# Sample scores of two key tiles per matmul with block-diagonal queries, V rows between half panels, masks ahead of the prompt scores, and two steps moved later

## The chip, the cores and the metric

The kernel runs on one core of one Trainium2 chip. The time is the device time of one execution in microseconds; the kernel before took 842.92 us (median of three runs, 841.31 to 843.15). Lower is better. The engines are TensorE (PE in the profile, with its weight loads as PEld), VectorE (DVE), ScalarE (ACT), GpSimd (POOL) and SyncE (SP), which issues most transfers.

## The reference

One layer of a hybrid attention encoder, for 512 prompt tokens and 64 sample tokens. Everything is fp32.

```python
qa, ka, va, qb, kb, vb, gates = split(rmsnorm(x, g_norm1) @ w_in)
oa = sliding_window_attention_with_sinks(qa, ka, va)          # 8 heads of 64, 2 key heads
z = einsum('bqhd,bkhd->bhqk', qb, kb) * HEAD_DIM ** -0.5      # stick-breaking, 8 heads of 64
mask = k_pos[None, :] < q_pos[:, None]
log_1m = where(mask, log_sigmoid(-z), 0)
tail = cumsum(log_1m, reverse=True) - log_1m
ob = einsum('bhqk,bkhd->bqhd', where(mask, exp(log_sigmoid(z) + tail), 0), vb)
merged = sigmoid(gate_a) * (oa @ w_proj_a) + sigmoid(gate_b) * (ob @ w_proj_b)
x = x + merged @ w_out
x = x + square(relu(rmsnorm(x, g_norm2) @ w_up)) @ w_down     # D_FF = 4096
y = rmsnorm(x, g_final)
```

The sample's stick-breaking attention (`sb_sample`) has 64 queries per head against 512 cached keys and the 64 new ones. The new K and V rows are outputs too.

## The kernel before

Activations lie transposed, features on the 128 partitions and the 576 tokens (512 prompt, 64 sample) along the free axis. A large product is a **panel**: 128 output features by 576 tokens, 8 contraction tiles of 128. Each operand is split into a high and a low fp32r part, and a contraction tile takes three products (high by high, high by low, low by high) over two halves of 288 tokens: 6 matmuls per contraction tile, 48 per panel (`mm3`, L1550). A `half_panel` has 4 contraction tiles, 24 matmuls. Each engine runs a program of its own written out by hand, and semaphores tie them together. `tile_out` counts finished panels in halves, `tile_taken` the panels that DVE has copied out of PSUM, `w_lo_ready` the panels whose weights are split.

**The sample's stick-breaking unit.** It runs twice (u = 0, 1), for four heads each time, after the input projection and between the half panels of the first output projection (panels 18 to 21). `sample_scores(u)` first adds a mask (a bf16 matmul of an identity with `smask`). Then, for each of the four heads, it multiplies 64 rows of keys by 64 columns of queries in plain fp32: 4 matmuls for the new keys and 16 for the cached keys `cKT` (4 key blocks by 4 heads). A feature tile of 128 partitions holds two heads, and u picks its upper or lower 64 partitions. Plain fp32 matmuls show as two records each in the trace. DVE and ACT then form magnitudes, exponentials, logarithms and high and low parts (`sp_hi`, `sp_lo`), PE sums them in `tails(u)`, ACT takes the exponential, and `sample_values(u)` multiplies by the V rows. In u = 0 the five groups of four transposes that make the **V rows** (`rows`, L1733) stand so: three groups directly behind the scores, the fourth (`v_rows(3)`) in the middle of half panel (18, 0), the fifth (`v_rows(4)`) before half panel (18, 1). ACT copies them to `vR` in `take_v_rows`, and SP stores `vR` and `kR` when all are there.

**The prompt units.** Eight units (four loops of two) follow, each with `prompt_scores(q)`, two panels, `tails` and the values. The scores are fp32r matmuls of 256, 384 or 512 columns, with bf16 mask matmuls of 128 or 256 columns between them. Three signals `z_out` tell DVE that a bank is complete.

**The second norm.** PE sums the squares by token (L1906), ACT and DVE form the root and DVE spreads it to a tile (`rrep2`); `spread_rms(2, rrep2)` (L1647) turns it with ten matmul records, and stands after 4 of the 8 contraction tiles of panel 51.

**The end.** The down projection is done in quarter products of 12 matmuls (`product`, L1766), which DVE adds to the residual in `take` steps. Output rows are transposed back in `x_rows_out` (L2023). In the last pair of tiles, `x_rows_out(2, 0)` stands between the first product (form 0) and the second (form 6).

Of the kernel before, what the change touches and what calls it, by code (L numbers as in the profile page):

```python
# [54 lines left out]
def build(nc, x_prompt, x_sample, cache_swa_k, cache_swa_v, cache_sb_k, cache_sb_v, rel_table, g1, w_in, sinks,  # L55
          w_pa, w_pb, w_out, g2, w_up, w_down, gf, consts, onehot, y_prompt, y_sample, p_swa_k, p_swa_v,
          p_sb_k, p_sb_v, s_swa_k, s_swa_v, s_sb_k, s_sb_v):
    with ExitStack() as ctx:
# [481 lines left out]
        def _(act):  # L540
# [153 lines left out]
            def sb_logs(u, order, wid):  # L694

                for n, bank in enumerate(order):
# [5 lines left out]
                    if isinstance(u, int) and u == 0 and n:  # L702
                        take_v_rows(n - 1)
# [31 lines left out]
            for u in range(2):  # L735
                sb_logs(u, SAMPLE_ORDER, SAMPLE_W)
                if u == 0:
                    take_v_rows(2)
                    take_v_rows(3)
                    take_v_rows(4)  # L740
                round_next(4, 2 * u)
                if u:
# [5 lines left out]
                nc.scalar.activation(ob_hi[u * HD:(u + 1) * HD, :, SEQ:TOK], att[0:HD, 3, 0:4 * NEW].rearrange("p (h n) -> p h n", h=4),  # L748
                                     ACT.Copy).then_inc(sbo_hi, 1)
# [153 lines left out]
        def _(dve):  # L903
# [252 lines left out]
            for u in range(2):  # L1156
# [20 lines left out]
                for n in range(1, 4):  # L1177
# [3 lines left out]
                nc.vector.tensor_tensor(ob_lo[u * HD:(u + 1) * HD, :, SEQ:TOK], att[0:HD, 3, 0:4 * NEW].rearrange("p (h n) -> p h n", h=4),  # L1181
                                        ob_hi[u * HD:(u + 1) * HD, :, SEQ:TOK].bitcast(F32), ALU.subtract).then_inc(sbo_taken, 1)
# [362 lines left out]
        def _(pe):  # L1545
# [598 lines left out]
```

## Time and profile before

| | |
|---|---|
| median of three runs | 842.92 us (841.31 to 843.15) |
| the profiled execution | 847.74 us |
| its span, first to last instruction | 845.9 us |
| mean granted TensorE clock | 0.989 |
| PE busy | 833.9 us, 99% of the span |
| DVE busy | 621.5 us, 73% |
| ACT busy | 391.2 us, 46% |
| POOL busy | 293.3 us, 35% |

The span ends with some 8 us in which PE has no more work: the last rows are scaled and stored. A row of a timeline gives start, duration, engine, line, operation, out<-in, shapes and how many records were merged. A matmul's duration holds a fixed part of its pipeline, so the cost of one in a row of alike records is the distance between starts. It is read as the row's duration less that of one record, divided by the number of records less one.

### The profile page before, as it was taken

How to read it: one execution, taken by the hardware profiler on the slowest of the kernel's cores; microseconds unless marked ns; L12 is line 12 of the kernel's file. 1: busy time of each engine (PE TensorE's matmuls, PEld its weight loads, DVE VectorE, ACT ScalarE, POOL GpSimd, SP SyncE). 2: the span in 40 equal slices, each digit the busy share in tenths (PEclk: the TensorE clock that was granted, in tenths of full speed). 3: DMA queues.
4: the chain of work that ended last, by engine and by line, in shares of the span. 5: the costliest groups of instructions: out<-in, count | busy, mean ns of one | idle time of the engine just before them, and what ended most of it. 6: DMA issues, size and time to landing. Idle time of an engine off the chain costs nothing.

```text
span 845.9 us, 16088 instructions
## 1 busy us (share of the span) xinstructions
PE 833.9 (99%) x6245; PEld 815.6 (96%) x6245; DVE 621.5 (73%) x1069; ACT 391.2 (46%) x666; POOL 293.3 (35%) x213
## 2 busy tenths in 40 slices
PE   9999999999999999999999999999999999999996
PEld 7999999999999999999999999999999999999995
DVE  5597876245688999967336889488975889489896
ACT  5667774233468677553343333323433333333532
POOL 2463222312535555245334400542025400452330
PEclk9999999988999999999999999999999999999998
DMA  8752112441111122143232213413133212322203
GB/s 278 253 166 72 51 51 66 147 162 51 51 51 50 50 71 79 50 162 117 60 99 87 65 50 100 149 52 96 51 100 107 92 50 93 120 84 61 87 2 113
DMA packets 68449, 78.18 MB, mean 92 GB/s; under 512 B 2552, under 2 KB 65072, under 8 KB 68016
## 3 DMA queue, kind: packets, MB, share of 16 engines
q1 hardware_dynamic: 68080, 76.92, 28.3%
q8 instruction: 32, 0.52, 0.3%
q10 hardware_dynamic: 320, 0.60, 0.2%
q14 instruction: 17, 0.14, 0.1%
HBM read 70.15 MB, written 8.93 MB: 93 GB/s over the span
## 4 chain that ended last, share of the span: by engine, by line
PE 91%; DVE 6%; issue 1%; ACT 1%; DMA 1%; ACTq 0%; DVEq 0%
PE pan L1550 58%; PE pan L1766 12%; PE att L1766 12%; PE att L1704 1%; PE att L1677 1%; PE pan L1606 1%; PE att L1694 1%; PE att L1550 1%; DVE xT L1383 1%; PE att L1845 1%; DMA grow<-in_g 1%; PE pan L1639 1%; PE att L1733 0%; DVE sq_sum L1482 0%; DVE x_out L1469 0%
## 5 line engine op out<-in xcount | busy, mean ns | idle before, releaser
L468 POOL TENSOR_TENSOR w_lo<-raw,w_hi 128x512 fp32r<-128x512 f32 x160 | 221.1, 1406 | 437.5 <-ACT w_hi L810 183.6
L1550 PE MATMUL pan<-a_hi,w_hi 128*128 128x288 f32 x624 | 134.3, 297 | 0.0
L1550 PE MATMUL pan<-a_lo,w_hi 128*128 128x288 f32 x624 | 133.8, 295 | 0.0
L1550 PE MATMUL pan<-a_hi,w_lo 128*128 128x288 f32 x624 | 133.2, 295 | 0.0
L1550 PE MATMUL pan<-h_hi,w_hi 128*128 128x288 f32 x512 | 111.1, 299 | 0.0
L1550 PE MATMUL pan<-h_lo,w_hi 128*128 128x288 f32 x512 | 109.5, 295 | 0.0
L1550 PE MATMUL pan<-h_hi,w_lo 128*128 128x288 f32 x512 | 108.3, 293 | 0.0
L1550 PEld LDWEIGHTS pan<-a_hi,w_lo 128*128 128x128 f32 x624 | 100.8, 188 | 0.0
L1550 PEld LDWEIGHTS pan<-a_hi,w_hi 128*128 128x128 f32 x624 | 99.4, 188 | 0.3
L1550 PEld LDWEIGHTS pan<-a_lo,w_hi 128*128 128x128 f32 x624 | 99.4, 188 | 0.0
L1766 PE MATMUL pan<-F_hi,w_hi 128*128 128x288 f32 x320 | 96.3, 301 | 0.0
L1766 PE MATMUL pan<-F_lo,w_hi 128*128 128x288 f32 x320 | 94.7, 296 | 0.0
L1766 PE MATMUL pan<-F_hi,w_lo 128*128 128x288 f32 x320 | 94.3, 295 | 0.0
L1550 PEld LDWEIGHTS pan<-h_lo,w_hi 128*128 128x128 f32 x512 | 83.7, 190 | 0.0
L1550 PEld LDWEIGHTS pan<-h_hi,w_lo 128*128 128x128 f32 x512 | 82.6, 188 | 0.0
L1550 PEld LDWEIGHTS pan<-h_hi,w_hi 128*128 128x128 f32 x512 | 81.2, 188 | 0.1
L1766 PEld LDWEIGHTS pan<-F_hi,w_hi 128*128 128x128 f32 x320 | 60.1, 188 | 1.2 <-DVE F_lo L1303 0.7
L1766 PEld LDWEIGHTS pan<-F_hi,w_lo 128*128 128x128 f32 x320 | 60.2, 188 | 0.0
L810 ACT ACTIVATE w_hi<-raw 128x1024 fp32r<-128x1024 f32 x28 | 29.7, 1061 | 65.8 <-PE pan L1550 43.9
L1766 PEld LDWEIGHTS pan<-F_lo,w_hi 128*128 128x128 f32 x320 | 60.1, 188 | 0.0
L1283 DVE TENSOR_TENSOR up_t<-pan,rms 128x576 f32<-128x576 f32 x32 | 24.1, 754 | 36.5 <-PE pan L1550 36.3
L545 ACT ACTIVATE w_hi<-raw 128x1024 fp32r<-128x1024 f32 x32 | 33.4, 1056 | 28.0 <-PE pan L1550 27.8
(281 smaller groups left out, 1790.1 us busy)
## 6 DMA issues: line engine op xcount, KB each, us to landing
raw<-in_w_in SPq DMA_DIRECT2D x34, 512.0 KB, 4.8
raw<-in_w_up SPq DMA_DIRECT2D x32, 512.0 KB, 4.5
raw<-in_w_down SPq DMA_DIRECT2D x32, 512.0 KB, 4.6
raw<-in_w_out SPq DMA_DIRECT2D x8, 512.0 KB, 4.0
x_spill<-xT SPq DMA_DIRECT2D x1, 2304.0 KB, 7.1
xT<-x_spill SPq DMA_DIRECT2D x1, 2304.0 KB, 10.6
x_rows<-in_x_prompt SPq DMA_DIRECT2D x4, 512.0 KB, 7.1
raw<-in_w_pa SPq DMA_DIRECT2D x4, 512.0 KB, 4.1
```

Source lines behind the costliest of these rows:

```text
L468: last = nc.gpsimd.tensor_tensor(w_lo[:, slot, k:k + 4, :], raw[:, rs, k:k + 4, j * P:(j + 1) * P], w_hi[:, slot, k:k + 4, :].bitcast(F32) ...
L545: nc.scalar.activation(w_hi[:, slot4(j), :, :], raw[:, 1 - j // 2, :, (j % 2) * P:(j % 2 + 1) * P], ACT.Copy).then_inc(w_hi_ready, 1)
L810: nc.scalar.activation(w_hi[:, slot4(n % 4), :, :], raw[:, 1 - n // 2 % 2, :, (n % 2) * P:(n % 2 + 1) * P], ACT.Copy).then_inc(w_hi_ready, 1)
L1283: nc.vector.tensor_tensor(halves(up_t[:, b, :]), pan_out(b), halves(rms[:]), ALU.mult).then_inc(tile_taken, 2)
L1383: nc.vector.tensor_tensor(xT[:, tile, cols], xT[:, tile, cols], bank, op).then_inc(taken, 1)
L1550: got = nc.tensor.matmul(out[:, h, 0:HALF], w, x[:, h * HALF:(h + 1) * HALF], start=first and n == 0, stop=last and n == 2)
L1606: nc.tensor.matmul(pan[:, j, h, 0:HALF], w_hi[:, j, k, :], x[:, k, h * HALF:(h + 1) * HALF], start=k == 0 and x is a_hi, stop=False)
L1639: got = nc.tensor.matmul(pan[:, j, h, 0:HALF], w_lo[:, j, k, :], a_hi[:, k, h * HALF:(h + 1) * HALF], start=False, stop=k == KT - 1)
L1677: got = nc.tensor.matmul(att[0:width(t), r, e * 256:(e + 1) * 256], qa_st[:, e, pair, t * P:t * P + width(t)], part[:, pair // 2, k0:k0 + ...
L1694: got = nc.tensor.transpose(att[0:kn, 2, c:c + w], s_sw[0:w, r, e, kb * P:kb * P + kn], ident[0:w, 0:w])
L1704: got = nc.tensor.matmul(att[0:HD, 3, 0:256].rearrange("p (e n) -> p e n", e=2)[:, :, 0:width(t)], va_st[0:kn, vt, g // 10, v_part, :], p_ ...
L1766: return nc.tensor.matmul(out, lhsT, rhs, start=start, stop=stop, skip_group_check=True)
```

## The change

- In `sample_scores` the four 64-row matmuls of a step become two 128-row ones. A new tile `qz` holds, for each of the four feature tiles, 128 columns: the 64 queries of the tile's first head on the upper 64 partitions with zeros below, and those of the second head on the lower 64 with zeros above. A unit now takes the two heads of two feature tiles (heads 4u to 4u+3) and not one head of each of four. DVE fills `qz` by two memsets and two copies, ahead of the copies of the K rows.
- The result of the values goes out in two pieces, on ACT and on DVE.
- The V rows: three groups in the middle of half panel (18, 0), the fourth before half panel (18, 1), the fifth in its middle. ACT takes the first later in its program.
- In `prompt_scores` all masks stand ahead of the scores.
- `spread_rms(2)` stands after 5 contraction tiles of panel 51.
- `x_rows_out(2, 0)` stands behind the form 6 product.

```diff
+        qz = work("qz", [P, 4, P], 98976)
+        def sample_out(e):
+            return att[0:HD, 3, 0:4 * NEW].rearrange("p (h e n) -> p e h n", h=2, e=2)[:, e, :, :]
@@ scalar
-                    if isinstance(u, int) and u == 0 and n:
-                        take_v_rows(n - 1)
+                    if isinstance(u, int) and u == 0 and n == 2:
+                        take_v_rows(0)
...
-                    take_v_rows(2)
-                    take_v_rows(3)
-                    take_v_rows(4)
+                    for n in range(1, TT + 1):
+                        take_v_rows(n)
...
-                nc.scalar.activation(ob_hi[u * HD:(u + 1) * HD, :, SEQ:TOK], att[0:HD, 3, 0:4 * NEW].rearrange("p (h n) -> p h n", h=4),
-                                     ACT.Copy).then_inc(sbo_hi, 1)
+                for e in range(2):
+                    last = nc.scalar.activation(ob_hi[e * HD:(e + 1) * HD, 2 * u:2 * u + 2, SEQ:TOK], sample_out(e), ACT.Copy)
+                last.then_inc(sbo_hi, 1)
@@ vector
             dve.wait_ge(stored, 6 * 16)
+            dve.wait_ge(tile_taken, 2 * KB)
+            for e in range(2):
+                own, other = slice(e * HD, (e + 1) * HD), slice((1 - e) * HD, (2 - e) * HD)
+                nc.vector.memset(qz[other, :, e * NEW:(e + 1) * NEW], 0.0)
+                last = nc.vector.tensor_copy(qz[own, :, e * NEW:(e + 1) * NEW], qkvT[own, QB:QB + 4, SEQ:TOK])
+            last.then_inc(qz_ready, 1)
...
@@ tensor, sample_scores
-                for h in range(4):
-                    got = acc(att[0:NEW, 2, h * NEW:(h + 1) * NEW], qkvT[rows, KB + h, SEQ:TOK], qkvT[rows, QB + h, SEQ:TOK], stop=h == 3)
+                for h in range(2):
+                    got = acc(att[0:NEW, 2, h * P:(h + 1) * P], qkvT[:, KB + 2 * u + h, SEQ:TOK], qz[:, 2 * u + h, :], stop=h == 1)
...
-                        for h in range(4):
-                            got = acc(att[:, bank, c % 512 + h * NEW:c % 512 + (h + 1) * NEW], cKT[rows, h, kb * P:(kb + 1) * P],
-                                      qkvT[rows, QB + h, SEQ:TOK], start=kb % 2 == 0 and h == 0, stop=kb % 2 == 1 and h == 3)
+                        for h in range(2):
+                            got = acc(att[:, bank, c % 512 + h * P:c % 512 + (h + 1) * P], cKT[:, 2 * u + h, kb * P:(kb + 1) * P],
+                                      qz[:, 2 * u + h, :], start=kb % 2 == 0 and h == 0, stop=kb % 2 == 1 and h == 1)
@@ tensor, half panels of u = 0
-                half_panel(18 + 2 * u, 0, slot4(2 * u), oa_hi, oa_lo, middle=None if u else lambda: v_rows(3))
+                half_panel(18 + 2 * u, 0, slot4(2 * u), oa_hi, oa_lo, middle=None if u else first_v_rows)
                 if u == 0:
-                    v_rows(4)
+                    v_rows(3)
                     pe.wait_ge(vrows_ready, 3)
-                half_panel(18 + 2 * u, 1, slot4(2 * u), oa_hi, oa_lo)
+                half_panel(18 + 2 * u, 1, slot4(2 * u), oa_hi, oa_lo, middle=None if u else lambda: v_rows(4))
@@ tensor, prompt_scores
-                qk(2, att[:, 1, 0:256], 256, start=True)
-                acc(att[:, 1, 0:P], ident_b[:], strict)
+                acc(att[:, 1, 0:P], ident_b[:], strict, start=True)
                 acc(att[:, 1, 256:512], ident_b[:], mask2[:])
+                acc(att[:, 2, 0:P], ident_b[:], strict, start=True)
+                acc(att[:, 0, 0:P], ident_b[:], strict, start=True)
+                qk(2, att[:, 1, 0:256], 256)
...
-            panel(first_panel(12) + 1, slot4(1), 1, h_hi, h_lo, part=(0, 4))
+            panel(first_panel(12) + 1, slot4(1), 1, h_hi, h_lo, part=(0, 5))
             spread_rms(2, rrep2)
...
             product(last_a, 2, 0, 0).then_inc(prod_out, 1)
-            x_rows_out(2, 0)
             last_taken(-2)
             pe.wait_ge(*quarter_low(3, 3, 3))
             product(att[:, 0, 0:HALF], 0, 0, 6).then_inc(prod_out, 1)
+            x_rows_out(2, 0)
```

PE's program before, at the scores of u = 0. `qkvT` holds queries, keys and values; L1766 is the helper of the scores, L1733 the V rows, L1550 the panels.

```order
L1766 MATMUL att<-smask,ident_b 128x256
L1766 MATMUL att<-qkvT 64x64 x4
L1766 MATMUL att<-qkvT,cKT 128x64 x16
L1733 MATMUL att<-ident,qkvT 64x128 x4
L1733 MATMUL pan<-ident,qkvT 128x128 x8
L1550 MATMUL pan<-oa_hi,w_hi 128x288 x2
L1550 MATMUL pan<-oa_lo,w_hi 128x288 x2
```

The same place in the changed kernel, where the three lines are L1781, L1748 and L1565.

```order
L1781 MATMUL att<-smask,ident_b 128x256
L1781 MATMUL att<-qz,qkvT 64x128 x2
L1781 MATMUL att<-qz,cKT 128x128 x8
L1565 MATMUL pan<-oa_hi,w_hi 128x288 x2
L1565 MATMUL pan<-oa_lo,w_hi 128x288 x2
L1565 MATMUL pan<-oa_hi,w_lo 128x288 x2
```

Twenty matmuls of 64 columns have become ten of 128 columns, and the twelve transposes behind them have gone; they follow after two contraction tiles (12 matmuls) of the half panel.

PE's program before, at the scores of a prompt unit (q_hi, q_lo and k_st are the parts of queries and keys, mask_60 the mask).

```order
L1766 MATMUL att<-q_hi_87,k_st_85 128x256
L1766 MATMUL att<-q_lo_89,k_st_85 128x256
L1766 MATMUL att<-mask_60,ident_b 128x128
L1766 MATMUL att<-mask_60,ident_b 128x256
L1766 MATMUL att<-q_hi_87,k_st_85 128x256
L1766 MATMUL att<-q_lo_89,k_st_85 128x256
L1766 MATMUL att<-q_hi_87,k_st_85 128x384
L1766 MATMUL att<-q_lo_89,k_st_85 128x384
L1766 MATMUL att<-mask_60,ident_b 128x128
L1766 MATMUL att<-q_hi_87,k_st_85 128x512
L1766 MATMUL att<-q_lo_89,k_st_85 128x512
L1766 MATMUL att<-mask_60,ident_b 128x128
```

And in the changed kernel.

```order
L1781 MATMUL att<-mask_60,ident_b 128x128
L1781 MATMUL att<-mask_60,ident_b 128x256
L1781 MATMUL att<-mask_60,ident_b 128x128 x2
L1781 MATMUL att<-q_hi_88,k_st_86 128x256
L1781 MATMUL att<-q_lo_90,k_st_86 128x256
L1781 MATMUL att<-q_hi_88,k_st_86 128x256
L1781 MATMUL att<-q_lo_90,k_st_86 128x256
L1781 MATMUL att<-q_hi_88,k_st_86 128x384
L1781 MATMUL att<-q_lo_90,k_st_86 128x384
L1781 MATMUL att<-q_hi_88,k_st_86 128x512
L1781 MATMUL att<-q_lo_90,k_st_86 128x512
```

The same twelve matmuls, with one change from bf16 to fp32r in place of three.

DVE's program before, where the K rows are copied (kR), between two copies of panels (L973).

```order
L1103 MEMSET vR 64x512
L1111 COPY kR<-att 128x512 x2
L973 SCALAR_TENSOR_TENSOR qkvT<-pan,qscale,rms 128x576
L1111 COPY kR<-att 128x512 x2
L1111 COPY kR<-att 64x512
```

And in the changed kernel.

```order
L1115 MEMSET qz 64x4x64
L1116 COPY qz<-qkvT 64x4x64
L1115 MEMSET qz 64x4x64
L1116 COPY qz<-qkvT 64x4x64
L1123 COPY kR<-att 128x512 x2
L979 SCALAR_TENSOR_TENSOR qkvT<-pan,qscale,rms 128x576
```

Four instructions of 64 partitions by 256 elements stand between the wait for the stores and the first copy of K rows.

## Rows read from the trace of the kernel before

**Rows 1.** The page: busy time, granted clock by slice, chain; longest piece of the chain.

```profile
PE 833.9 (99%) x6245; PEld 815.6 (96%) x6245; DVE 621.5 (73%) x1069; ACT 391.2 (46%) x666; POOL 293.3 (35%) x213
...
PEclk9999999988999999999999999999999999999998
...
PE 91%; DVE 6%; issue 1%; ACT 1%; DMA 1%; ACTq 0%; DVEq 0%
...
364.59 82.74 PE pan L1550 x624
```

**Rows 2.** Windows: length, busy by engine (PE first), then granted clock, DMA, GB/s.

```profile
168.50:169.00 0.50, 0.50 (x7) 0.50 (x5) 0.40 (x1) 0.07 (x1) 0.50 (x1) 0.87 0.00 0
169.00:169.50 0.50, 0.50 (x4) 0.50 (x4) 0.00 (x0) 0.50 (x2) 0.23 (x1) 0.50 0.00 0
...
175.50:176.00 0.50, 0.50 (x5) 0.50 (x5) 0.47 (x2) 0.00 (x0) 0.00 (x0) 0.81 0.12 33
...
196.00:196.50 0.50, 0.50 (x5) 0.50 (x5) 0.27 (x1) 0.20 (x1) 0.50 (x1) 0.67 0.00 0
...
203.00:203.50 0.50, 0.50 (x5) 0.50 (x5) 0.02 (x1) 0.00 (x0) 0.00 (x0) 1.00 0.00 0
```

**Rows 3.** Timeline of PE at both sample scores.

```profile
165.35 0.28 PE L1766 MATMUL att<-smask,ident_b 128*128 128x256 bf16 x1
...
166.17 4.66 PE L1766 MATMUL att<-qkvT,cKT 64*128 64x64 f32 x32
170.76 1.06 PE L1733 MATMUL att<-ident,qkvT 128*64 128x128 f32 x4
...
192.73 0.28 PE L1766 MATMUL att<-smask,ident_b 128*128 128x256 bf16 x1
...
198.20 0.85 PE L1550 MATMUL pan<-oa_hi,w_hi 128*128 128x288 f32 x2
```

**Rows 4.** Timeline of PE, plain fp32 records with all 128 rows.

```profile
161.29 1.03 PE L1751 MATMUL att<-ident,ckR 128*128 128x128 f32 x8
...
189.19 0.63 PE L1845 MATMUL att<-sp,cV 128*64 128x64 f32 x8
```

**Rows 5.** Timeline of DVE where `qz` is to be filled.

```profile
146.63 1.29 DVE L1111 COPY kR<-att 128x512 f32<-128x512 f32 x2 [2.21 <-DMA out_s_swa_v<-vaR]
149.83 0.82 DVE L973 SCALAR_TENSOR_TENSOR qkvT<-pan,qscale,rms 128x576 f32<-128x576 f32 x1 [1.91 <-PE pan L1550]
```

**Rows 6.** Timeline of DVE in u = 1: third magnitude, copy of panel (20, 0).

```profile
198.31 0.69 DVE L1125 TENSOR_SCALAR sp<-att 128x512 int32<-128x512 int32 x1 [2.04 <-PE att L1766]
...
203.83 0.76 DVE L1160 COPY m_a<-pan 128x576 f32<-128x576 f32 x1 [0.81 <-PE pan L1550]
```

**Rows 7.** Timeline of PE in a prompt unit, behind a mask matmul.

```profile
219.00 0.48 PE L1766 MATMUL att<-q_hi,k_st 128*128 128x512 f32 x1
219.32 0.40 PE L1766 MATMUL att<-q_lo,k_st 128*128 128x512 f32 x1
```

**Rows 8.** PE's longest wait in the prompt units; waits of PEld (us, times, longest).

```profile
321.56 0.44 PE L1766 MATMUL att<-sp_hi,suffix 128*128 128x384 f32 x1 [0.74 <-DVE sp_lo L1147]
...
PEld att L1766 <- DVE sp_lo L1147: 1.8, 6, 0.9
```

**Rows 9.** Timeline of PE at the second norm's spread.

```profile
451.27 0.42 PE L1550 MATMUL pan<-h_hi,w_lo 128*128 128x288 f32 x2
...
452.17 1.52 PE L1647 MATMUL att<-ident,rrep 128*128 128x128 f32 x10 [0.48 <-DVE rrep L960]
```

**Rows 10.** Timelines of PE and DVE at the last pair.

```profile
823.09 0.65 PE L2023 MATMUL att<-ident,xT 128*128 128x128 f32 x4 [1.01 <-DVE xT L1383]
...
825.18 0.29 PE L1766 MATMUL pan<-F_hi,w_hi 128*128 128x288 f32 x1
...
822.59 0.45 DVE L1383 TENSOR_TENSOR xT<-xT,pan 128x288 f32<-128x288 f32 x1
...
824.22 0.45 DVE L1383 TENSOR_TENSOR xT<-xT,pan 128x288 f32<-128x288 f32 x1
```

More of the change, by code:

```diff
@@ L202, in build @@
         krows_out, vrows_out, vrows_ready, krows_ready = sem("krows_out"), sem("vrows_out"), sem("vrows_ready"), sem("krows_ready")
+        qz_ready = sem("qz_ready")
         csb_in, ckT_out, ckT_ready = sem("csb_in"), sem("ckT_out"), sem("ckT_ready")
@@ L1180, in _ @@
                 dve.wait_ge(stored, (6 + 4) * 16)
-                nc.vector.tensor_tensor(ob_lo[u * HD:(u + 1) * HD, :, SEQ:TOK], att[0:HD, 3, 0:4 * NEW].rearrange("p (h n) -> p h n", h=4),
-                                        ob_hi[u * HD:(u + 1) * HD, :, SEQ:TOK].bitcast(F32), ALU.subtract).then_inc(sbo_taken, 1)
+                for e in range(2):
+                    own = slice(e * HD, (e + 1) * HD)
+                    last = nc.vector.tensor_tensor(ob_lo[own, 2 * u:2 * u + 2, SEQ:TOK], sample_out(e), ob_hi[own, 2 * u:2 * u + 2, SEQ:TOK].bitcast(F32),
+                                                   ALU.subtract)
+                last.then_inc(sbo_taken, 1)
             def take_gate(i, j):
@@ L1768, in sample_scores @@
             def sample_scores(u):
-                rows = slice(u * HD, (u + 1) * HD)
                 acc(att[:, 2, 0:4 * NEW], ident_b[:], smask[:], start=True)
-                for h in range(4):
-                    got = acc(att[0:NEW, 2, h * NEW:(h + 1) * NEW], qkvT[rows, KB + h, SEQ:TOK], qkvT[rows, QB + h, SEQ:TOK], stop=h == 3)
+                for h in range(2):
+                    got = acc(att[0:NEW, 2, h * P:(h + 1) * P], qkvT[:, KB + 2 * u + h, SEQ:TOK], qz[:, 2 * u + h, :], stop=h == 1)
                 got.then_inc(z_out, 1)
@@ L1813, in _ @@
                     pe.wait_ge(ckT_ready, 4)
+                    pe.wait_ge(qz_ready, 1)
                 else:
@@ L1816, in _, with first_v_rows @@
                 sample_scores(u)
-                if u == 0:
+                def first_v_rows():
                     pe.wait_ge(tile_taken, 2 * QKV)
@@ L1840, in sample_values @@
                     for h in range(4):
-                        c = (2 * h + u) * HD
+                        c = (4 * u + h) * HD
                         for kb in range(5):
@@ L1858, in prompt_scores @@
                 strict = mask2[:, P:2 * P]
-                qk(2, att[:, 1, 0:256], 256, start=True)
-                acc(att[:, 1, 0:P], ident_b[:], strict)
+                acc(att[:, 1, 0:P], ident_b[:], strict, start=True)
                 acc(att[:, 1, 256:512], ident_b[:], mask2[:])
+                acc(att[:, 2, 0:P], ident_b[:], strict, start=True)
+                acc(att[:, 0, 0:P], ident_b[:], strict, start=True)
+                qk(2, att[:, 1, 0:256], 256)
                 qk(3, att[:, 1, 256:512], 256, stop=True).then_inc(z_out, 1)
-                qk(1, att[:, 2, 0:384], 128, start=True)
-                acc(att[:, 2, 0:P], ident_b[:], strict, stop=True).then_inc(z_out, 1)
-                qk(0, att[:, 0, :], 0, start=True)
-                acc(att[:, 0, 0:P], ident_b[:], strict, stop=True).then_inc(z_out, 1)
+                qk(1, att[:, 2, 0:384], 128, stop=True).then_inc(z_out, 1)
+                qk(0, att[:, 0, :], 0, stop=True).then_inc(z_out, 1)
             pe.wait_ge(tile_taken, 44)
@@ L1912, in _ @@
             feature_sums(1)
-            panel(first_panel(12) + 1, slot4(1), 1, h_hi, h_lo, part=(0, 4))
+            panel(first_panel(12) + 1, slot4(1), 1, h_hi, h_lo, part=(0, 5))
             spread_rms(2, rrep2)
-            panel(first_panel(12) + 1, slot4(1), 1, h_hi, h_lo, part=(4, KT))
+            panel(first_panel(12) + 1, slot4(1), 1, h_hi, h_lo, part=(5, KT))
             for n in range(2, 8):
```

## The prediction

> **What bounds the kernel now.** I read the page first: busy shares, granted clock by slice, the chain that ended last. PE is busy for 833.9 us, 99% of the span, and holds 91% of the chain [rows 1]. So a microsecond counts if PE loses or gains it, and the work of the others matters only where PE waits for it. The same group gives the yardstick: a run of 624 panel matmuls takes 82.74 us, 0.1326 us each, so 12 take 1.59 us and a half panel of 24 takes 3.18 us.
>
> Next, the clock. The row by slice dips in slices 9 and 10, and again in the last, where PE's work is over [rows 1]. Windows of half a microsecond place the two dips. With PE busy 0.50 of 0.50, the granted clock is 0.87 in the window from 168.50 and 0.50 in the next, so it fell at 168.87; by 0.81 in the window from 175.50 it rose at 175.69. It fell again at 196.17 and was back at 203.00 [rows 2]. That is twice 6.8 us at 1.2 GHz instead of 2.4. The timeline shows what PE did before each fall: sample scores, from 165.35 and from 192.73, thus 3.5 us of matmuls that fill 64 rows of the array [rows 3].
>
> **Sample scores: fewer records.** At u = 0 the scores last from 165.35 to 170.76, 5.41 us; at u = 1 from 192.73 to 198.20, 5.47 us [rows 3]. The clock was halved for 1.89 and 2.03 us of these, so at full clock they are 4.46 and 4.45 us. Now the new form. No row shows a 128-row fp32 score of 128 columns. The nearest are the transposes with all 128 rows and 128 columns: eight records in 1.03 us, the last 0.27, so (1.03 - 0.27) / 7 = 0.109 us apart [rows 4]. The low side is the fp32 records of 64 weight columns in the values: (0.63 - 0.22) / 7 = 0.059 [rows 4]. The old scores' cached part gives the high side: 32 records in 4.66 us with 1.89 at half clock, so (4.66 - 0.27 - 0.95) / 31 = 0.111 for only 64 columns [rows 3]; twice that for twice the columns would be 0.22. I take 0.109, since both operands have the transposes' shape. With 4 + 16 records for 8 + 32: 0.22 for the mask + 20 x 0.109 = 2.40 us. PE gains 2.06 + 2.05 = **4.1 us**, between 0 (0.22 a record) and 6.1.
>
> **Sample scores: the clock.** If it stays up, each 6.8 us stretch becomes 3.4 us: **6.8 us** in both. The reason to think so: the new scores are shorter (2.4 us against 3.5 us before the fall), fill all 128 rows, and panel matmuls follow them (at u = 0 twelve transposes did). Also, the values are a stretch of fp32 records too, 40 of them at 0.059 each, 2.4 us with all rows filled [rows 4], and ended shortly before the second scores without a fall before 196.17 [rows 2]. Bounds: 0 to 6.8.
>
> The Trainium skill, in "TensorE: Matmul & The Clock Gate" (Part 1: The HAM clock gate), says that the clock is granted by how busy the array has been and falls after an idle stretch. The falls here came with PE busy in all of every window [rows 2], so busy in the profile's sense isn't what is counted. By the page's wording, scores that keep PE just as busy in their new form would be treated as before, and the clock term is 0, which is a rival below.
>
> **What the filling of `qz` costs.** Four DVE instructions of 64 partitions by 256 elements. A copy of 128x512 takes 0.64 us by two in 1.29 [rows 5]; half the columns is about 0.3, so 1.2 in all. DVE starts the K rows at 146.63, and before the next panel copy at 149.83 it was idle for 1.91 us [rows 5], which covers it; PE needs `qz` some 17 us later. Cost 0; without the cover the K copies come 1.2 us late and PE would wait up to that.
>
> **V rows, and the waits behind the scores.** The twenty transposes stay the same. With the scores 2.1 us shorter and the clock up, PE reaches everything behind them earlier, and DVE and ACT must follow. For u = 0 I set out the chain with the durations above: scores end at 167.75, two contraction tiles, V rows to 170.6, and so on to the tails at 179.5; DVE's copy of half panel (18, 0) waits for the fifth V group. Behind that PE has 12 panel matmuls, 1.59 us, before it needs the bank, and the copy takes 0.76 [rows 6]: some 0.5 us to spare, signals included. The splits then have the whole half panel (19, 0), 3.18 us. No wait. For u = 1 it is tighter. Half panel (21, 0) needs the copy of (20, 0). Before, DVE started the third magnitude at 198.31 and that copy at 203.83, of which 0.81 was idle: 4.71 us of work [rows 6]. Now the magnitudes come right behind the two result pieces: the third starts 3.3 us after the scores start, so the copy ends at 3.3 + 4.7 + 0.76 = 8.8 us. PE is there at 2.40 + 2 x 3.18 = 8.76. I take a **loss of 0.1 us**, 0 to 0.7.
>
> **Masks ahead.** A matmul behind a mask shows 0.48 us against 0.40 for the same shape behind fp32r [rows 7]: its weight load isn't hidden, 0.08. Three such changes a unit become one. The wide mask's costs about nothing, so one 0.08 goes, and a unit that begins behind a wait starts with a cheaper bf16 load. That is 0.1 us x 8 units. But in three units DVE, late by its own backlog, ends the wait (0.74 us at 321.56, and 1.8 us in 6 times [rows 8]), and what PE saves ahead of such a wait is given back. Five units: **0.5 us**, 0 to 0.9. The first signal `z_out` comes 0.2 us later, the last earlier; where DVE is late it isn't waiting for it.
>
> **The norm's spread.** The last two panel records start at 451.27 and end their slot at 451.53, the spread starts at 452.17 [rows 9]: 0.64 us lost. Six more matmuls are 0.80, so the spread would start at 452.33 with `rrep2` there. **0.6 us**, 0.4 at least. DVE gets its result 0.17 us later, and PE needs the tile it frees only a panel later.
>
> **The last row transposes.** PE waits 1.01 us for DVE's `take` that starts at 822.59, and the third product starts at 825.18 [rows 10]. In the new order form 6 runs in that gap, from 821.93 to 823.5, the transposes to 824.0. The third product then waits for the take that starts at 824.22, DVE being busy throughout, and ends at 824.67 [rows 10]: it starts at 824.7. **0.45 us** and not 1.0, range 0.2 to 1.0. The wait moves from the transposes to the product.
>
> **Sum.** 4.1 + 6.8 + 0.5 + 0.6 + 0.45 - 0.1 = 12.35 us. Against its own time the profiled execution goes from 847.74 to 835.4. It was 4.8 us above the median of the runs, 842.92; the same gain gives **830.6 us**.
>
> **Rivals.** (1) The clock term is missing (20%): it falls again, or it fell in the profiled execution alone. For: the page's rule above, and the 4.8 us between profile and median. Against: the three runs lie within 1.84 us, so none of them differs from the rest by two such falls, and the shorter scores fill the array. Gain 5.55: 837.4 us. With one of two falls left, 834.0.
> (2) DVE and ACT don't follow, and their chain from the scores to the splits sets the start of the tails (7%). The scores and the clock give PE 5.5 us in each unit, all of it ahead of the tails. If one unit's chain kept its old times, 5.5 of it would be lost: 836.1 us. For: the chain is long, with 4.71 us of DVE work behind the third signal of u = 1 [rows 6], and has only 0.1 us or less to spare there. Against: its inputs are PE's results, which all move.
> (3) Slower (3%): the 128-column records are the price, and the clock falls as before. The old scores' records took 0.111 us, and twice that at half clock. If a record of the new shape took 0.25, a unit's scores would be 0.22 + 20 x 0.25 = 5.2 us, 0.75 more than 4.45, twice 1.5, and the 1.45 of the three small edits would be gone: from there the change loses. At 0.32 it is 842.92 + 2 x 2.15 - 1.45 = 845.8 us. Against: the 0.109 of the transposes [rows 4].
>
> The change could also fail to do what it says only in the three small edits, which the range holds.
>
> **Chances.** Forecast with its own range (829.3 to 832.5) 68%, rival (1) 20%, rival (2) 7%, rival (3) 3%, better than 829.3 2%. A range from 829.2 to 837.5 holds some 85%, and the unknown costs reach across it. A difference of 0.2% (1.7 us) is about what a measurement can tell from no change. Only rival (3), and a mix of both (1) and (2), come near that: faster 0.95, same 0.03, slower 0.02.
>
> **What would show it.** In the new profile: granted clock 1.00 from 165 to 200 us (term of 6.8); score stretches of 2.4 us, with records 0.109 apart; tails of u = 0 near 179.5; a wait of PE by DVE's copy before half panel (21, 0) of at most 0.2 us; one slow fp32r matmul a prompt unit, with the waits for `sp_lo` at 0.1 more each; no idle PE before the spread; 0.7 us of idle PE between the last transposes and the third product. Clock windows at 0.50 behind the new scores would make the forecast wrong by 3.4 us each, score records above 0.15 by 0.8 us or more.

## The result and the profile after

The changed kernel takes **836.17 us** (median of four runs, 836.07 to 836.72). Beside it the kernel before took 843.03 (four runs, 841.31 to 843.46), a ratio of 0.9913 with a 95% interval of 0.9887 to 0.994. The gain is 6.9 us. The forecast was 830.6 us: the sign was right, the result lies in the wide range (829.2 to 837.5), and the likeliest value was 5.6 us too low. Yet the two profiled executions differ by 847.74 - 836.16 = 11.58 us, close to the forecast sum of 12.35.

The page after: busy time, clock by slice, the chain by engine (to [rows 1]).

```profile
PE 822.9 (99%) x6205; PEld 807.0 (97%) x6205; DVE 624.6 (75%) x1075; ACT 391.4 (47%) x668; POOL 294.6 (35%) x213
...
PEclk9999999999999999999999999999999999999998
...
PE 88%; DVE 9%; issue 2%; ACT 1%; DVEq 0%; ACTq 0%
```

PE is busy for 11.0 us less, and the dip of slices 9 and 10 is gone. Windows of 5 us around the scores of u = 0 and behind those of u = 1 (columns as in [rows 2]) have the clock at 1.00:

```profile
165.00:170.00 5.00, 5.00 (x41) 4.61 (x40) 2.95 (x5) 3.17 (x6) 2.52 (x2) 1.00 0.00 0
170.00:175.00 5.00, 5.00 (x43) 5.00 (x41) 3.08 (x6) 3.02 (x6) 0.00 (x0) 1.00 0.66 210
...
193.00:198.00 5.00, 5.00 (x39) 4.83 (x38) 4.79 (x10) 1.66 (x3) 0.00 (x0) 1.00 0.63 210
```

PE's timeline in the same execution, from the scores to the tails of both units, the first prompt unit, the norm's spread and the last pair (to [rows 3, 7, 9, 10]):

```profile
165.59 0.28 PE L1781 MATMUL att<-smask,ident_b 128*128 128x256 bf16 x1
165.80 0.65 PE L1781 MATMUL att<-qz,qkvT 128*64 128x128 f32 x4
166.38 2.05 PE L1781 MATMUL att<-qz,cKT 128*128 128x128 f32 x16
168.19 0.51 PE L1565 MATMUL pan<-oa_hi,w_hi 128*128 128x288 f32 x2
...
169.86 0.60 PE L1748 MATMUL att<-ident,qkvT 128*64 128x128 f32 x4
...
179.96 0.28 PE L1781 MATMUL att<-sp_hi,suffix 128*128 128x256 f32 x1
...
187.94 0.28 PE L1781 MATMUL att<-smask,ident_b 128*128 128x256 bf16 x1
...
201.40 0.28 PE L1781 MATMUL att<-sp_lo,prefix 128*128 128x256 f32 x1
201.69 0.39 PE L1781 MATMUL att<-sp_hi,suffix 128*128 128x256 f32 x1
...
208.47 0.45 PE L1781 MATMUL att<-mask,ident_b 128*128 128x128 bf16 x4
208.72 0.36 PE L1781 MATMUL att<-q_hi,k_st 128*128 128x256 f32 x1
...
442.42 1.41 PE L1662 MATMUL att<-ident,rrep 128*128 128x128 f32 x10
443.76 0.53 PE L1565 MATMUL pan<-h_hi,w_hi 128*128 128x288 f32 x2
...
812.53 0.60 PE L2039 MATMUL att<-ident,xT 128*128 128x128 f32 x4
813.73 0.40 PE L1781 MATMUL pan<-F_hi,w_hi 128*128 128x288 f32 x1 [0.59 <-DVE xT L1398]
```

The scores take 2.6 us (165.59 to 168.19), and their cached records are (2.05 - 0.27) / 15 = 0.119 us apart. The tails of u = 0 begin 14.37 us behind the mask that opens the scores; in the profile of before it was 19.4. Inside the tails of u = 1 there is a new gap at 201.69, where matmuls otherwise follow 0.12 us apart. The spread has no wait in front of it, and in the last pair 0.59 us of wait stand ahead of the third product. So the profile shows nearly what was forecast. Why did the time not show it?

### The profile page after: what moved, and what is told of

Read it like the earlier page. It is cut to its first block, busy times and chain, and to the rows that moved or that the text cites. A ratio compares the mean times of both kernels' runs of the same rounds, so it can differ in the third digit from the quotient of the medians.

```text
span 834.3 us, 16017 instructions
## 1 busy us (share of the span) xinstructions
PE 822.9 (99%) x6205; PEld 807.0 (97%) x6205; DVE 624.6 (75%) x1075; ACT 391.4 (47%) x668; POOL 294.6 (35%) x213
## 4 chain that ended last, share of the span: by engine, by line
PE 88%; DVE 9%; issue 2%; ACT 1%; DVEq 0%; ACTq 0%
PE pan L1565 56%; PE pan L1781 12%; PE att L1781 10%; PE att L1719 1%; PE att L1692 1%; PE pan L1621 1%; DVE sp_lo L1159 1%; PE att L1709 1%; PE att L1565 1%; DVE sp_hi L1157 1%; DVE xT L1398 1%; PE pan L1601 1%; PE att L1861 1%; PE pan L1654 1%; DVE ob_lo L1221 1%
## 5 line engine op out<-in xcount | busy, mean ns | idle before, releaser
L1565 PE MATMUL pan<-a_lo,w_hi 128*128 128x288 f32 x624 | 133.8, 295 | 0.0
L1565 PE MATMUL pan<-a_hi,w_hi 128*128 128x288 f32 x624 | 133.8, 296 | 0.0
L1565 PE MATMUL pan<-a_hi,w_lo 128*128 128x288 f32 x624 | 133.1, 294 | 0.0
L1565 PE MATMUL pan<-h_hi,w_hi 128*128 128x288 f32 x512 | 110.5, 298 | 0.0
L1565 PE MATMUL pan<-h_lo,w_hi 128*128 128x288 f32 x512 | 109.5, 295 | 0.0
L1565 PE MATMUL pan<-h_hi,w_lo 128*128 128x288 f32 x512 | 108.5, 293 | 0.0
L1565 PEld LDWEIGHTS pan<-a_hi,w_hi 128*128 128x128 f32 x624 | 99.9, 188 | 1.0
L1565 PEld LDWEIGHTS pan<-a_hi,w_lo 128*128 128x128 f32 x624 | 100.8, 188 | 0.0
L1565 PEld LDWEIGHTS pan<-a_lo,w_hi 128*128 128x128 f32 x624 | 99.6, 188 | 0.0
L1781 PE MATMUL pan<-F_hi,w_hi 128*128 128x288 f32 x320 | 96.4, 301 | 0.6 <-DVE xT L1398 0.6
L1781 PE MATMUL pan<-F_lo,w_hi 128*128 128x288 f32 x320 | 94.7, 296 | 0.0
L1781 PE MATMUL pan<-F_hi,w_lo 128*128 128x288 f32 x320 | 94.3, 295 | 0.0
L1565 PEld LDWEIGHTS pan<-h_lo,w_hi 128*128 128x128 f32 x512 | 83.2, 189 | 0.0
L1565 PEld LDWEIGHTS pan<-h_hi,w_lo 128*128 128x128 f32 x512 | 82.7, 188 | 0.0
L1565 PEld LDWEIGHTS pan<-h_hi,w_hi 128*128 128x128 f32 x512 | 81.4, 188 | 0.1
L1781 PEld LDWEIGHTS pan<-F_hi,w_hi 128*128 128x128 f32 x320 | 60.1, 188 | 2.0 <-DVE xT L1398 1.1
L1781 PEld LDWEIGHTS pan<-F_hi,w_lo 128*128 128x128 f32 x320 | 60.2, 188 | 0.0
L1781 PEld LDWEIGHTS pan<-F_lo,w_hi 128*128 128x128 f32 x320 | 60.1, 188 | 0.0
```

The lines of the kernel that those rows point to most:

```text
L1565: got = nc.tensor.matmul(out[:, h, 0:HALF], w, x[:, h * HALF:(h + 1) * HALF], start=first and n == 0, stop=last and n == 2)
L1781: return nc.tensor.matmul(out, lhsT, rhs, start=start, stop=stop, skip_group_check=True)
```

## Experiments

Each was timed beside the kernel before. All times are medians, with the lowest and the highest. A **fall** is a stretch in which the granted clock is half (1.2 GHz in place of 2.4).

### 1. The kernel before, unchanged

No edit.

> The kernel before, unchanged, to see the clock of each of its executions. Theory A (the two stretches at half clock belong to some executions, the profiled one among them; most timed ones have none or one, or shorter ones): the mean granted clock of most executions is above the 0.989 of the profiled one, up to the 0.996 of the kernel after, and span and clock move together, 1% of clock for some 8 us of span; executions without a fall take 840.9 us (847.74 - 6.8), with one fall 844.3. Theory B (every execution has both falls): the clock is 0.989 in all of them, whatever their time, and the 4.8 us between the profiled execution and the median are something else.

**Measured:** 843.59 us (841.98 to 847.80, 12 runs), against 843.46 for before: ratio 1.001 (0.9986 to 1.0033). With the runs of before beside all the experiments there are 99 executions of this one kernel, with the span and the mean clock of each. They form three groups:

| executions | time | median | mean granted clock |
|---|---|---|---|
| 13 | 841.18 to 842.02 | 841.63 | 0.996 to 0.997 |
| 53 | 842.59 to 844.70 | 843.30 | 0.993 to 0.996 |
| 33 | 846.23 to 848.74 | 847.63 | 0.988 to 0.991 |

The profiled execution of this run was one of the middle group (843.17 us). Its windows of half a microsecond show one fall only, and that a short one:

```profile
170.00:170.50 0.50, 0.50 (x6) 0.43 (x6) 0.17 (x1) 0.20 (x1) 0.00 (x0) 0.99 0.00 0
170.50:171.00 0.50, 0.50 (x5) 0.46 (x3) 0.50 (x2) 0.00 (x0) 0.00 (x0) 0.50 0.57 59
...
173.50:174.00 0.50, 0.50 (x4) 0.50 (x4) 0.45 (x2) 0.50 (x2) 0.00 (x0) 0.60 1.08 367
174.00:174.50 0.50, 0.50 (x6) 0.50 (x6) 0.45 (x2) 0.21 (x1) 0.00 (x0) 1.00 0.43 131
```

It lasts from 170.5 to 173.9, 3.4 us at half rate, and costs 1.7: the distance between the first two medians (843.30 - 841.63). The two falls of [rows 2] cost 6.8 by their rows; the third median lies 6.0 above the first. Only single executions were profiled; that the others of a group had the same falls is read from their time and mean clock. Theory A holds and theory B falls. Theory A allowed for shorter falls, but had no time for them, and they are the commonest: a short fall at u = 0, and none at u = 1.

The u = 1 of this execution is undisturbed, and so gives what no row of before could. From the chain of the end (start, length, line):

```profile
191.70 4.44 PE att L1766 x41
196.15 9.72 PE pan L1550 x72
...
211.17 2.48 PE att L1845 x40
...
215.51 6.54 PE pan L1550 x49
```

### 2. The new scores alone

```diff
+        qz = work("qz", [P, 4, P], 98976)
...
-                for h in range(4):
-                    got = acc(att[0:NEW, 2, h * NEW:(h + 1) * NEW], qkvT[rows, KB + h, SEQ:TOK], qkvT[rows, QB + h, SEQ:TOK], stop=h == 3)
+                for h in range(2):
+                    got = acc(att[0:NEW, 2, h * P:(h + 1) * P], qkvT[:, KB + 2 * u + h, SEQ:TOK], qz[:, 2 * u + h, :], stop=h == 1)
```

> The kernel before with the block-diagonal sample scores alone (qz, 128-row score records, the outputs' head order); V rows, masks, spread and last rows as before. Both theories: the scores' stretch is 2.69 us as in the kernel after, against 4.45 at full clock, so 1.76 a unit, 3.5 us in both. Theory A (the records are a real gain, and the 6.8 us of the clock are a gain only against executions that had the falls): clock 0.996 in every execution, time about 837.4 (840.9 - 3.5), 5.5 us under the median of before and over 10 us under its profiled time. Theory C (the move of the V rows is what keeps the clock up, not the scores' form): clock falls to half behind the scores of u = 0 or u = 1 still, mean clock 0.993 or less, time 840 or more.

**Measured:** 838.08 us (837.89 to 838.46, 7 runs), ratio 0.992 (0.9891 to 0.9949), clock 0.996 or 0.997 in every execution. The V rows stand in their old place, so theory C falls. Against executions of before without a fall (called undisturbed from here on) the gain is 841.63 - 838.08 = 3.55 us, against the median of all some 5.4.

### 3. All but the scores

```diff
-                for h in range(2):
-                    got = acc(att[0:NEW, 2, h * P:(h + 1) * P], qkvT[:, KB + 2 * u + h, SEQ:TOK], qz[:, 2 * u + h, :], stop=h == 1)
+                for h in range(4):
+                    got = acc(att[0:NEW, 2, h * NEW:(h + 1) * NEW], qkvT[rows, KB + h, SEQ:TOK], qkvT[rows, QB + h, SEQ:TOK], stop=h == 3)
```

(against the kernel after; the cached part and the outputs likewise)

> The kernel after with the old sample scores (64-row records, no qz): V rows between steps, masks ahead, spread and last rows later are as in after. Theory A: the three small edits give 1.5 us (0.5 masks, 0.6 spread, 0.45 last rows) and the V rows nothing, so executions without a fall take 839.4 us, and falls behind the scores are as frequent as in before. Theory C (the V rows keep the clock up): no fall in any execution, clock 0.996, 839.4 in all. If the V rows' place costs PE something by itself, the time is above 839.4 at clock 0.996.

**Measured:** 843.52 us (839.85 to 846.13, 12 runs), ratio 0.9988 (0.9963 to 1.0014). Only two executions kept 0.997 (839.85 and 839.99); the profiled one has a fall from 168.4 to 175.3, which began before its scores ended at 171.2. The four other edits without the scores bring 1.7 us to an undisturbed execution, and don't hold the clock.

### 4. The three small edits alone

```diff
-            panel(first_panel(12) + 1, slot4(1), 1, h_hi, h_lo, part=(0, 4))
+            panel(first_panel(12) + 1, slot4(1), 1, h_hi, h_lo, part=(0, 5))
```

(with the masks' and the last rows' edits as in the change)

> The kernel before with the three small edits alone: masks ahead of the prompt scores, the second norm's spread two panel steps later, the last row transposes behind form 6. By the rows of the two traces: masks 0.4 to 0.5 us, spread 0.6, last rows 0.45, together 1.5 us, so 1.5 under a run of before with the same clock (839.4 without a fall). Rival: later waits take the masks' share back, and the sum is 1.0. A difference to the kernel after's gain of more than 5.4 us is then the scores' and the clock's.

**Measured:** 842.01 us (839.81 to 847.09, 12 runs), ratio 0.9983 (0.9958 to 1.0009); its two executions at 0.997 took 839.81 and 839.94. That is again 1.7 us under 841.63, and the same as experiment 3: the V rows' move is worth nothing measurable, as far as two executions of each can tell.

### 5. All 128 rows, but as many matmuls as before

```diff
-                for h in range(2):
-                    got = acc(att[0:NEW, 2, h * P:(h + 1) * P], qkvT[:, KB + 2 * u + h, SEQ:TOK], qz[:, 2 * u + h, :], stop=h == 1)
+                for h in range(4):
+                    k, e = 2 * u + h // 2, slice(h % 2 * NEW, (h % 2 + 1) * NEW)
+                    got = acc(att[0:NEW, 2, h * NEW:(h + 1) * NEW], qkvT[:, KB + k, SEQ:TOK], qz[:, k, e], stop=h == 3)
```

(against experiment 2; the cached part likewise)

> The block-diagonal kernel of the run before (all else as in before), with each score matmul cut into two of 64 query columns, so that the array's 128 rows are filled but there are as many records as in before (8 and 32 a unit). Price: if a record costs by its columns, 40 x 0.06 = 2.4 us a unit and the time is 838; if a record costs the same 0.11 whatever the columns, the scores take 4.45 us as in before, 3.5 us more than with 20 records, 841.4 at full clock. Clock: theory R (the 64 rows are what let it fall): clock 0.996 in every execution. Theory L (the length of the fp32 stretch is what lets it fall, however many rows): falls as in before, in most executions, mean clock down to 0.989, times spread over 6 us.

**Measured:** 841.38 us (841.05 to 841.65, 12 runs), ratio 0.9962 (0.9946 to 0.9979), clock 0.996 to 0.998 in all twelve. The cached scores in PE's timeline, and below them those of the undisturbed u = 1 of experiment 1, with 64 rows:

```profile
166.31 3.79 PE L1782 MATMUL att<-qz,cKT 128*128 128x64 f32 x32
...
192.36 3.78 PE L1766 MATMUL att<-qkvT,cKT 64*128 64x64 f32 x32
```

This is the experiment that decides. The stretch is as long as before (4.45 us), with as many matmuls, and of the scores only the rows differ (half of the 128 meet the zeros of `qz`). By time and mean clock 86 of 99 executions with 64 rows have a fall, 21 of the 23 timed beside this experiment, and of 12 with 128 rows none. And it prices the record: (3.79 - 0.27) / 31 = 0.114 us with 64 query columns, whether 128 rows are filled or 64, and 0.119 with 128. Half the matmuls at 128 columns are therefore nearly half the time, 841.38 - 838.08 = 3.3 us.

### 6. As few matmuls, but 64 rows

```diff
-                    got = acc(att[0:NEW, 2, h * P:(h + 1) * P], qkvT[:, KB + 2 * u + h, SEQ:TOK], qz[:, 2 * u + h, :], stop=h == 1)
+                    got = acc(att[0:NEW, 2, h * P:(h + 1) * P], qkvT[0:HD, KB + 2 * u + h, SEQ:TOK], qz[0:HD, 2 * u + h, :], stop=h == 1)
```

(against experiment 2; the cached part likewise)

> The block-diagonal kernel with the score matmuls cut to the first 64 rows: 20 records a unit of 64 rows and 128 columns (every second head's scores are left out, so the output differs). Both theories: 2.69 us a unit as with 128 rows, 838.0 us if the clock holds. Theory R (64 rows): the clock can fall, some executions 2 to 7 us longer with mean clock 0.989 to 0.995. Theory L (length): as short as the block-diagonal form, so no fall in any execution, and all within 1 us of 838.0.

**Measured:** 838.16 us (837.74 to 838.50, 6 runs), ratio 0.9923 (0.9894 to 0.9951), clock 0.996 or 0.997 in all six. No fall: 64 rows for 2.7 us did not bring one. So theory R in its plain form (64 rows are enough) is not borne out. But this edit changes two things against the kernel before: the stretch is shorter, and each matmul has 128 query columns in place of 64. Which of the two kept the clock up is not separated here. Six executions don't exclude a rare fall either.

### 7 and 8. Both kinds of scores issued twice

```diff
+                sample_scores(u, False)
                 sample_scores(u)
```

> The block-diagonal kernel with every score matmul of the sample issued twice (the first pass is written over): 2 x 2.69 = 5.4 us of 128-row fp32 scores a unit, longer than the old ones' 4.45. Theory R: no fall, clock 0.996 in every execution, time 838.0 + 5.4 = 843.4 with a spread of 1 us. Theory L: falls in at least as many executions as in before, 845 to 850 us, clock down to 0.989.

> The kernel before with every score matmul of the sample issued twice (the first pass is written over): 8.9 us of 64-row scores a unit at full clock. Both theories: the clock falls more often or for longer than in before: without a fall it would be 841.3 + 8.9 = 850.2 us, with one or two 853 to 858 us, and the shortest executions, those without a fall, become rare or go. If the times stay near 850.2 at clock 0.996, neither rows nor length of the scores is the cause.

**Measured, 128 rows:** 843.29 us (842.65 to 843.62, 12 runs), ratio 0.9985 (0.9966 to 1.0003), clock 0.996 to 0.998 in all: 5.36 us of fp32 records with all rows filled, longer than the old scores, and no fall.

**Measured, 64 rows:** 862.49 us (859.96 to 863.21, 6 runs), ratio 1.0201 (1.017 to 1.0233), clock 0.981 to 0.985: a long fall in every execution. Both have the same place in the kernel, but not the same length. The windows of the profiled execution with 64 rows:

```profile
169.50:170.00 0.50, 0.50 (x7) 0.50 (x6) 0.00 (x0) 0.00 (x0) 0.03 (x1) 1.00 0.00 0
170.00:170.50 0.50, 0.50 (x5) 0.31 (x5) 0.00 (x0) 0.00 (x0) 0.00 (x0) 0.89 0.00 0
...
184.00:184.50 0.50, 0.50 (x6) 0.50 (x5) 0.47 (x2) 0.00 (x0) 0.00 (x0) 0.96 0.00 0
```

The clock is at half from 170.4 to 184.0, with PE busy 0.50 of 0.50, and again from 204.5 to 218.2. I had expected 853 to 858: each fall is 13.6 us long here and costs 6.8, and two of them with the 8.9 us of matmuls make 841.6 + 8.9 + 13.6 = 864, which is near the 863.07 of this execution.

### 9 and 10. The new gap in the tails of u = 1

DVE in the kernel after, third addition and split of u = 1:

```profile
196.20 0.75 DVE L1172 COPY m_a<-pan 128x576 f32<-128x576 f32 x1
...
198.50 1.43 DVE L1157 CAST sp_hi<-sp 128x512 fp32r<-128x512 f32 x1
199.97 1.67 DVE L1159 TENSOR_TENSOR sp_lo<-sp,sp_hi 128x512 fp32r<-128x512 f32 x1
201.56 1.41 DVE L1172 COPY m_a<-pan 128x576 f32<-128x576 f32 x2
```

The same two operations took 0.43 and 0.69 us one bank earlier. POOL at that time:

```profile
198.37 2.72 POOL L474 TENSOR_TENSOR w_lo<-raw,w_hi 128x512 fp32r<-128x512 f32 x2 [6.52 <-ACT w_hi L551]
```

PE waits for `sp_lo`, which ends at 201.64. The first edit (9) moves the work that lets POOL start:

```diff
-                round_next(4, 2 * u)
-                if u:
+                if u == 0:
+                    round_next(4, 0)
+                else:
                     stage_high(0, 0)
                 sb_weights(u, SAMPLE_ORDER, SAMPLE_W)
+                if u:
+                    round_next(4, 2)
```

The second (10) adds, on DVE:

```diff
-                        if n == 2:
-                            take_proj(4)
                         added = sb_add(u, n, SAMPLE_ORDER, SAMPLE_W, SAMPLE_ADDS, added)
+                        if n == 1:
+                            take_proj(4)
                         sb_split(u, n, SAMPLE_ORDER, SAMPLE_W)
```

> The kernel after with one move on ACT: at u = 1 the rounding of the next weight panel (w_hi, at 197.23) stands behind the tails' exponentials and not ahead of them, so POOL's split of that panel (198.37, 2.72 us) comes some 6 us later. Theory P (DVE's sp_hi and sp_lo at 198.50 took 1.43 and 1.67 us in place of 0.43 and 0.69 because POOL's split ran beside them): both are back at 0.43 and 0.69, PE's wait inside the tails of u = 1 (201.40 to 201.69) is gone, and PE gains 0.2 us: 835.9 against 836.17. Rival: the two are slow for another reason and stay at 1.4 and 1.7, or the later rounding costs PE a wait for w_lo at panel 22, over 836.2.

> The same, and DVE's copy of half panel (20, 0) one step earlier, ahead of the second split and not of the third addition. If PE's wait of 0.18 us ahead of half panel (21, 0) (its 72 matmuls take 9.72 us in place of 9.53) is for that copy alone, the piece takes 9.53, and the second split ends 0.7 us later without PE noticing: 0.4 us under the kernel after with both moves, 835.8. Rival: the bank is late by something else and the piece stays at 9.7; then 835.95.

**Measured:** 839.80 us (838.50 to 840.46, 12 runs) with the first, 839.81 (838.25 to 841.33, 12 runs) with both: ratios 0.9951 (0.9934 to 0.9968) and 0.9939 (0.9918 to 0.9959). Both are 3.3 us slower than the kernel after (836.48 on the same chip, experiment 11), where a gain of 0.2 to 0.4 was expected. The splits are back at 0.43 and 0.69 us, so theory P is right in what it says of DVE, but its gain is swamped: POOL's chain to `q_lo` comes late for the first prompt unit. PE in the profiled executions of 9 and of 10, then the windows of 10 there:

```profile
210.63 0.45 PE L1784 MATMUL att<-mask,ident_b 128*128 128x128 bf16 x4 [2.57 <-POOL q_lo L497]
...
210.23 0.71 PE L1784 MATMUL att<-mask,ident_b 128*128 128x128 bf16 x4 [2.56 <-POOL q_lo L497]
```

```profile
208.00:209.00 1.00, 0.00 (x0) 0.00 (x0) 0.56 (x2) 0.97 (x3) 1.00 (x2) 1.00 0.00 0
209.00:210.00 1.00, 0.00 (x0) 0.00 (x0) 0.00 (x0) 0.99 (x2) 1.00 (x1) 0.88 0.00 0
210.00:211.00 1.00, 0.77 (x5) 0.71 (x6) 0.00 (x0) 0.07 (x1) 0.92 (x2) 0.50 0.00 0
```

PE waits for 2.56 us in 10, and before it resumes at 210.23 the clock falls, this time with PE idle: the 12 score matmuls behind the wait take 3.12 us. In the profiled execution of 9 the wait is as long (2.57 us) and there is no fall: the same 12 take 1.79 us. So one and the same wait can bring a fall or not. By the mean clock there was one in 8 of 12 executions of 10 (0.994 or 0.995, 839.53 us and more; the other four, at 0.996, took 838.25 to 838.87), and in at least 5 of 12 of 9.

### 11 and 12. The kernel after again, and the two moves with POOL in time

```diff
+                if u:
+                    act.wait_ge(tile_out, 2 * (first_panel(4) + 6) - 6)
+                    stage_high(0, 0)
                 round_next(4, 2 * u)
-                if u:
-                    stage_high(0, 0)
```

(experiment 12, with the DVE edit of 10)

> The kernel after, unchanged, beside the other two on the same chip: 836.2 us with the clock at 0.996 in every execution, since the 128-row scores do not let it fall; all within 0.7 us. If a fall shows in one of them (clock under 0.995, 838 us or more), the 128 rows only make it rarer.

> The kernel after with two moves at u = 1: ACT makes the parts of k_st and q_hi first (behind the wait for the same half panel as before) and rounds the weight panel behind them, so POOL's split starts at about 200.2 and not 198.4, and its q_lo for the first prompt unit ends near 206.9, ahead of the 208.4 at which PE wants it; DVE copies half panel (20, 0) ahead of the second split. Theory P (POOL beside DVE's splits stretched them, and the copy alone held up half panel (21, 0)): DVE's sp_hi and sp_lo are at 0.43 and 0.69 us, the 72 matmuls take 9.53 and not 9.72, no wait inside the tails, and the start of the first prompt unit keeps its time behind the values: 0.2 + 0.2 = 0.4 us under after's 836.2 to 836.5, so 835.9. Rival: as in the two moves tried before, POOL's chain to q_lo comes late and PE waits for it; then 836.5 or more, and a wait of 1 us or more lets the clock fall as well.

**Measured:** the kernel after took 836.48 us (836.08 to 836.80, 6 runs), ratio 0.9912 (0.9883 to 0.994), clock 0.996 to 0.998. The version of 12 took **835.85 us** (835.61 to 835.93, 6 runs), ratio to before 0.9897 (0.9871 to 0.9924). Its slowest execution is faster than the fastest of after's ten, but it ran on another chip than any of these, so the traces must carry the comparison: from the start of the scores of u = 0 to the panels of the first prompt unit the chain takes 44.05 us here and 44.51 in the kernel after. Its DVE and its chain:

```profile
198.31 0.43 DVE L1158 CAST sp_hi<-sp 128x512 fp32r<-128x512 f32 x1
198.78 0.69 DVE L1160 TENSOR_TENSOR sp_lo<-sp,sp_hi 128x512 fp32r<-128x512 f32 x1
```

```profile
190.59 9.52 PE pan L1566 x72
200.11 2.13 PE att L1782 x18
202.24 3.17 PE pan L1566 x24
205.41 2.48 PE att L1862 x40
207.88 1.72 PE att L1782 x12
```

POOL's split now starts at 199.94, behind DVE's. The piece of 72 is back at 9.52, the gap is gone, and the prompt unit follows the values without a wait.

## Why the forecast was right and where it failed

**The step that failed** is the last of the sum: "the same gain gives 830.6 us". It carried the profiled execution's gain over to the median. The clock term of 6.8 us was read rightly from its rows and is gone as forecast; but by time and mean clock only a third of the executions of before (33 of 99) lose about that much. The median one has the short fall of 1.7. Put that in place of 6.8 and the sum of the forecast is 7.25, 835.7 us. The profile's own 4.8 us above the median said so, and I had it in rival (1), "it fell in the profiled execution alone", at 20%. What I held against it was that the three runs lie within 1.84 us, "so none of them differs from the rest by two such falls". That is true, and also what one sees if none of the three has them. The result, 836.17, lies nearer to rival (1)'s 837.4 than to the forecast, and it is in the stated range only because the range reached out to that rival. That it meets rival (2)'s 836.1 is chance: the 5.5 us that rival (2) takes away were to be lost to DVE and ACT in one unit, and the kernel after loses 0.27 there.

**Score records.** I took 0.109 us, the transposes' distance; it is 0.119. The undisturbed old scores of experiment 1 are 4.44 us in the chain against 2.69 now: 1.75 a unit, 3.5 for 4.1. The low bound of 0.059 was out of reach: it belongs to records with 64 weight columns and 64 moving ones. The first V group has 64 weight columns too, but 128 moving ones, and takes (0.60 - 0.27) / 3 = 0.11.

**Why the clock stays up.** "Fill all 128 rows" was right: shown by 5 against 1. Experiment 7 bears it out, since 5.36 us with 128 rows are longer than the old scores' 4.45 and brought no fall; against 8 it differs in rows and in length. "Shorter" is in part argued. With one and the same form of matmul, 4.4 us (1) mostly brought a fall and 8.9 us (8) a long one each time. But 6, the only run with 64 rows and a short stretch, has 128 query columns a matmul as well; a stretch of 2.7 us in the old form was not run. The panel matmuls behind the scores matter little: in 3 they stand there too, and the clock fell before PE reached them. By the Trainium skill ("TensorE: Matmul & The Clock Gate", Part 1: The HAM clock gate) the clock goes by how busy the array has been, and falls behind an idle stretch. The trace of experiment 10 agrees, with a fall in a wait of 2.56 us, and that of 9 shows a wait of 2.57 us without one. In experiment 8 the clock fell with PE busy 0.50 of 0.50, so the busy time of the profile does not foretell it, and there the measurement decides.

**The wait at (21, 0).** Forecast 0.1. The piece of 72 takes 9.72, where 9.53 is without a wait, so the wait is 0.2. But it is 9.72 in the undisturbed u = 1 of experiment 1 too, so as a difference it is nothing.

**What I did not have** is the gap inside the tails: from the 72 matmuls' end at 200.50 to the next half panel at 202.90 it is 2.40 us, with 2.13 in experiment 12. I had costed DVE's splits at the durations of before. Moved earlier, the third met POOL's split of the next panel. It is a mechanism in the spirit of rival (2), at 0.27 us and not 5.5. Shown by 9, 10 and 12: with the overlap gone, both splits are back at 0.43 and 0.69 us. The Trainium skill, in "SBUF — State Buffer" ("Who interferes with whom"), names a port pair that DVE and POOL share, as a lock that one holds for its whole instruction. The trace agrees for the two splits (1.43 and 1.67 us beside POOL's); DVE's copy from PSUM beside POOL's `w_lo` wasn't slowed (two in 1.52 us from 199.39 in experiment 12, with POOL's split from 199.94).

**Masks ahead.** Forecast 0.5. The first unit starts its panels 1.72 us behind the values in place of 1.86, and from there to the run of 624 it is 144.43 us in place of 144.88: 0.6 in all. As forecast, part is given back where DVE is late: waits of PEld for `sp_lo`, 1.8 us in 6 times in experiment 1's profile, are now

```profile
PEld att L1781 <- DVE sp_lo L1159: 2.7, 8, 1.0
```

**Spread.** Forecast 0.6. From the end of the 624 to the same amount of work it is 5.60 us in place of 6.36: 0.76.

**Last rows.** Forecast 0.45, with 0.7 of wait left. The wait is 0.59. From the last `sq_sum` (DVE L1482) in the chain to the start of PE's last 12 matmuls it is 834.23 - 820.37 = 13.86 us in the profile of before and 13.49 in the kernel after, 13.85 in experiment 1 and 13.49 in 4: 0.37.

**V rows and `qz`.** Nothing, as forecast (3 against 4). The filling of `qz` costs PE nothing visible: in experiment 5, with `qz`, the undisturbed time is that of before.

**The sum by the runs.** 3.5 - 0.27 + 0.6 + 0.76 + 0.37 = 4.96 us, against 841.63 - 836.17 = 5.5 between undisturbed executions (5.15 by the later runs of after, 836.48); the rest to 6.9 is the clock, 843.03 - 841.63 = 1.4 in the runs of the result and 1.7 between the medians of the first two groups. Some 0.2 to 0.5 us are within the spread of undisturbed executions, and stay unassigned.

## What to carry to other kernels

Before a term read from one profiled execution goes into a forecast of the median, ask whether that execution is a median one: if its time and mean clock lie off the timed runs, the term may be its own. Stretches of fp32 matmuls that fill half the rows (4.4 us here) can take the clock down while PE looks fully busy, so filling the rows can save time beside that of the matmuls it spares. And when work moves earlier by microseconds, lay the other engines' timelines over its new place: a split that cost 0.4 us may meet another engine's, and moving that one in turn has a deadline of its own (3.3 us lost in 9; some 0.5 won in 12, by the traces).

## What the runs showed of the hardware

- The clock's falls had lengths of 3.4, 6.8 and 13.6 us in these traces, always at half rate, and executions of the same kernel showed a short one or two of 6.8, or by their mean clock none.
- An fp32 record with 128 weight columns costs 0.114 us with 64 moving columns and 0.109 (transposes) to 0.119 (scores) with 128; filling 64 rows in place of 128 doesn't change it. With 64 weight columns it costs 0.11 with 128 moving columns and 0.059 with 64 [rows 4]. So it was cheaper only where both sides had 64 columns.
- In a wait of 2.56 us of idle PE the clock fell in the profiled execution of 10, and by the mean clock in 8 of 12; in that of 9 it did not fall in 2.57 us.
- Two DVE splits, SBUF to SBUF, took 1.43 and 1.67 us beside POOL's subtractions, in place of 0.43 and 0.69.
